# Token rows of the first expert step by products with zero-one tiles instead of a gather

## The chip, the core and the metric

The kernel runs on one core of one Trainium2 chip. The metric is the device time of one execution in microseconds (us). A core has five engines that run beside each other and wait for each other by semaphores: TensorE (PE in the profile; PEld is its weight load), VectorE (DVE), ScalarE (ACT), GpSimd (POOL) and SyncE (SP). Here SP issues the loads of weights, POOL the loads and stores of token rows and of modulation vectors. All transfers run on the core's 16 DMA engines.

## What is computed

One step of a two-layer streaming encoder over 512 prompt tokens and 32 sample tokens, width 1024, all in float32. Each layer ends in a mixture of experts: 16 experts in 4 groups, two experts for each token, both from its best group.

```python
def _moe(h, w_router, b_router, w_gate, w_up, w_down):
    logits = jnp.einsum('btd,de->bte', h.astype(jnp.float32), w_router.astype(jnp.float32))
    scores = jax.nn.softmax(logits, axis=-1)
    ...
    for e in range(N_EXPERTS):
        act = jax.nn.silu(h @ w_gate[e]) * (h @ w_up[e])
        term = combine[..., e:e + 1] * (act @ w_down[e])
        y = term if y is None else y + term
    return y
```

The first layer's mixer pools over trailing tokens, the second's is attention over shared keys and values. Between them lie projections; in front of all of it, products of the conditioning vector with the adaLN weights give shift, scale and gate vectors.

## The kernel before

**Tiles.** The 544 tokens are `NT` = 5 tiles of 128 rows (the last has 32). `h` holds the normed tokens, one token to a partition. `pb[0..7]` are the PSUM banks.

**Routing.** `pick` on DVE finds each token's two experts; PE (`ranks`) counts, and DVE (`places`) computes from the counts the row of each token in a list sorted by expert. These row numbers are `posf[:, 0, r, t]` (r is the first or second expert, t the tile) and, cast to integers, `posi`; with the cast the semaphore `rows_ready` rises. `places` then goes on with tables (which expert stands where, which rows belong to a step, the rows to gather results from) and ends with `pos_ready`.

**Dispatch.** On POOL, `dispatch` waits for `rows_ready` and scatters `h` into the list `xs_d` in device memory by ten indirect transfers (`scattered`). After that and `pos_ready` it loads the rows of a step: `load_x(n)` brings 128 rows of `xs_d` into `xg[n % 2]`.

**Expert loop.** 13 steps (`NSTEP`) in each layer, with 128 rows of one expert or 64 rows each of two experts (`PATTERN`: B is one expert, P two). For a step, PE transposes the rows (`pe_tx`, into `pb[0]` and `pb[1]`), ACT and DVE copy one half each into `xgT` (`copy_x`), and PE multiplies by the gate weights, the up weights, transposes the activations and multiplies by the down weights. PE's order is written out in `experts`: up of step n, transposes and half of the gate of step n+1, transposed activations of n, the other half of the gate, down of n. Steps are numbered g through both layers.

**Order on each engine.** Each engine runs its instructions in the order of the code. On DVE that is `pick`, `places`, in the first layer three additions `stage_ada` for the last adaLN groups, then the loop's copies. On PE in the first layer the last adaLN groups, `ada(5)` and `ada(6)`, stand behind `ranks`, and the loop begins when `ada_staged` says that the last of them is added. On SP the weights of the first two steps come first; in the first layer the last four of these six loads wait until the rows of step 1 have landed (`xg_loaded[1]`). Later loads go into slots of `ring` as PE frees them.

**Memory that is shared.** `xg`, `xgT`, `sg` and `hact` lie over `h`: they may be written once the scatter has read it. `mod` holds the modulation vectors of a stage; `load_ab(2)` fills it for the next stage, with five loads on POOL.

The gather in `dispatch`, which the change moves and cuts:

```python
pool.wait_ge(scattered, 16 * 2 * NT * (layer + 1))
pool.wait_ge(pos_ready, layer + 1)
b = layer * NSTEP
load_x(0)
load_x(1)
if layer == 0:
    load_ab(2)
```

and the wait on SP in the first layer: `if layer == 0 and n == 2: sp.wait_ge(xg_loaded[1], 16)`.

Of the kernel before, what the change touches and what calls it, by code (L numbers as in the profile page):

```python
# [12 lines left out]
def bass_yoco_stream_step(  # L13
# [96 lines left out]
    with ctx:  # L110
# [26 lines left out]
        hactT = hT_raw[:, 0:512].rearrange("p (k t) -> p k t", k=KE)  # L137
        ysb = hT_raw[:, 512:2560].rearrange("p (b n) -> p b n", b=2)
        pair_w = hT_raw[:, 2560:3072].rearrange("p (a i j) -> p a i j", a=2, i=NE)

# [12 lines left out]
        partT_f = rf[:, 13312:13312 + TOK]  # L153
        mf = mod[:, :, :, :].rearrange("p a s d -> p (a s d)")
        PT = rf[:, 23552:24576].rearrange("p (b n) -> p b n", b=2)

# [127 lines left out]
        rows_ready = sem("rows_ready")  # L284
        pos_ready = sem("pos_ready")
        scattered = sem("scattered")
        xg_loaded = [sem(f"xg{i}_loaded") for i in range(2)]
# [225 lines left out]
        def _(pool):  # L513
# [102 lines left out]

            def dispatch(layer):
                pool.wait_ge(rows_ready, layer + 1)
                pool.wait_ge(tail_stored, 16)
# [17 lines left out]
                b = layer * NSTEP  # L637
                load_x(0)
                load_x(1)
                if layer == 0:  # L640
                    load_ab(2)

                for n in range(NSTEP):
                    if layer == 0 and n == NSTEP - 2:
                        for j in range(0, NOV, TP):
                            m = min(TP, NOV - j) * P
                            g.dma_start(ys_d[(NSTEP + j) * P:(NSTEP + j) * P + m, :], x_prompt[0, 0:m, :]).then_inc(rows_filled, 16)
                    if n + 2 < NSTEP:
                        pool.wait_ge(E.tx, 2 * (b + n) + 2)
                        load_x(n + 2)  # L650
                    pool.wait_ge(E.ys_act, b + n + 1)
                    pool.wait_ge(E.ys_dve, b + n + 1)
                    par = (b + n) % 2
                    g.dma_start(ys_d[n * P:n * P + P, :], ysb[:, par, :]).then_inc(y_stored[par], 16)  # L654
# [75 lines left out]
        def _(pe):  # L730
# [74 lines left out]
            def pe_tx(g, par):  # L805

                for half, done in enumerate((E.xt_act, E.xt_dve)):
# [4 lines left out]
                    last.then_inc(E.tx, 1)  # L812

            def tile_product(bank, lhs, rhs, start, stop):

                if len(rhs) == 1:
                    return T.matmul(bank[:, :], lhs, rhs[0], start=start, stop=stop)  # L817
                for a in range(2):
                    last = T.matmul(bank[HALF * a:HALF * a + HALF, :], lhs[:, HALF * a:HALF * a + HALF], rhs[a],  # L819
                                    start=start, stop=stop, tile_position=(0, HALF * a))  # L820
                return last

            def pe_gate(g, par, ws, ks):
                for k in ks:
                    if k == 0:
                        pe.wait_ge(E.xt_act, g + 1)
                        pe.wait_ge(E.xt_dve, g + 1)
                        if g:
                            pe.wait_ge(E.silu, g)
                    last = tile_product(pb[3], xgT[:, par, k, :], [w[:, k * DE:(k + 1) * DE] for w in ws],  # L830
                                        k == 0, k == KC - 1)
# [3 lines left out]
            def pe_up(g, par, ws):  # L835
                if g:
                    pe.wait_ge(E.hact, g)
                for k in range(KC):
                    last = tile_product(pb[4], xgT[:, par, k, :], [w[:, k * DE:(k + 1) * DE] for w in ws],
                                        k == 0, k == KC - 1)  # L840
                last.then_inc(E.up, 1)

            def pe_th(g):
                pe.wait_ge(E.hact, g + 1)
                for c in range(KE):
                    last = T.transpose(pb[2][:, c * P:(c + 1) * P], hact[:, c:DE:KE], ident[:, :])
                last.then_inc(E.th, 1)
# [12 lines left out]
            def experts(layer):  # L860
# [8 lines left out]
                def tokens(n):  # L869
                    g = b + n  # L870
                    loads = sum(len(STEP_PLACES[i % NSTEP]) for i in range(g % 2, g + 1, 2))
                    pe.wait_ge(xg_loaded[g % 2], 16 * loads)
                    pe_tx(g, g % 2)

                tokens(0)
                pe_gate(b, b % 2, units(G_SLOT, 0), range(KC))
# [267 lines left out]
        def _(act):  # L1144
# [84 lines left out]
            def experts(layer):  # L1229
                b = layer * NSTEP  # L1230

                def copy_x(g):
                    act.wait_ge(E.tx, 2 * g + 1)
                    if g >= 2:
                        act.wait_ge(E.up, g - 1)
                    A.activation(xgT[:, g % 2, 0:4, :], pb[0][:, :].rearrange("p (c t) -> p c t", c=4),  # L1236
                                 ACT.Copy).then_inc(E.xt_act, 1)

                copy_x(b)
                for g in range(b, b + NSTEP):  # L1240
                    act.wait_ge(E.gate, g + 1)
                    if g:
                        act.wait_ge(E.hact, g)
                    A.activation(sg, pb[3][:, :], ACT.Silu).then_inc(E.silu, 1)
                    if g + 1 < b + NSTEP:
# [200 lines left out]
        def _(dve):  # L1446
# [162 lines left out]
            def places(layer):  # L1609
# [20 lines left out]
                tt(selv[:, :, :], rank[:, :, :], bc(offs[:, :], NT, 1), ALU.add)  # L1630
                picked(0, selv).then_inc(rows_ready, 1)


# [50 lines left out]
            def experts(layer):  # L1684
                b = layer * NSTEP

                def copy_x(g):
                    dve.wait_ge(E.tx, 2 * g + 2)
                    if g >= 2:
                        dve.wait_ge(E.up, g - 1)  # L1690
                    V.tensor_copy(xgT[:, g % 2, 4:8, :], pb[1][:, :].rearrange("p (c t) -> p c t", c=4)).then_inc(E.xt_dve, 1)  # L1691

                copy_x(b)
                for g in range(b, b + NSTEP):
                    dve.wait_ge(E.silu, g + 1)
                    dve.wait_ge(E.up, g + 1)
                    if g:
                        dve.wait_ge(E.th, g)
                    V.tensor_tensor(hact, pb[4][:, :], sg, ALU.mult).then_inc(E.hact, 1)  # L1699
                    if g + 1 < b + NSTEP:  # L1700
# [309 lines left out]
```

## Time and profile before

| what | value |
|---|---|
| median of 3 runs | 1463.25 us (1459.91 to 1463.81) |
| the profiled execution | 1463.11 us |
| its span in the trace | 1461.6 us |
| PE busy | 1168.8 us, 80% of the span |
| DVE busy | 447.4 us, 31% |
| ACT busy | 237.4 us, 16% |
| POOL busy | 148.0 us, 10% |
| chain that ended last | PE 71%, DVE 12%, DMA 9%, issue 3% |
| DMA | 365 MB, mean 250 GB/s |

The page lists busy time by engine, the span in slices, the queues, the chain of work that ended last and the costliest groups of instructions. A busy share is a mean over stages with different limits; what a stage is worth is read from the chain and the timeline of that stage. In a group, "out<-in" names the tiles; the last part is the idle time of the engine just before, with what ended most of it. `h<-xs_d` is the load of token rows: `xg` lies in `h`. Line 811 is the transposes of the rows, 817 and 819 the expert products (one or two experts), 744 the adaLN products, 1691 DVE's copy of the transposed rows.

### The profile page before, as it was taken

The numbers are of one execution on the slowest core, as the hardware profiler recorded it, in microseconds if no ns is written. First come the engines' busy times: TensorE is split into PE (matmuls) and PEld (weight loads), VectorE is DVE, ScalarE is ACT, GpSimd is POOL, SyncE is SP. The second block draws the span as 40 slices with busy tenths as digits, with TensorE's granted clock in tenths as the row PEclk, the third lists the DMA queues.
The fourth block names the chain that finished last, engine by engine and source line by source line (L and its number), as shares of the span: only waits on it lengthen the run. The fifth ranks groups of instructions, "written<-read, shape, count | busy, mean of one in ns | idle before, by whom it ended". The sixth has DMA issues, their size and how long they took to land.

```text
span 1461.6 us, 13678 instructions
## 1 busy us (share of the span) xinstructions
PE 1168.8 (80%) x4952; PEld 605.7 (41%) x4952; DVE 447.4 (31%) x1023; ACT 237.4 (16%) x517; POOL 148.0 (10%) x280
## 2 busy tenths in 40 slices
PE   2559748899999965999995888779934999999990
PEld 0027314344344422444554777555422444344340
DVE  1144640001010018264146677222363000101005
ACT  2002101010101004112123444211120001010101
POOL 6100030000000011000003000201003000000002
PEclk9869868999999986999997899779966999999996
DMA  9999799999998972311425000817035799899835
GB/s 320 400 388 353 272 403 380 392 430 348 386 402 331 381 274 80 109 58 61 181 58 161 0 0 0 253 55 298 0 133 205 282 421 379 354 428 346 346 135 197
DMA packets 55233, 365.44 MB, mean 250 GB/s; under 512 B 7215, under 2 KB 7711, under 8 KB 36156
## 3 DMA queue, kind: packets, MB, share of 16 engines
q1 hardware_dynamic: 32512, 285.79, 49.9%
q0 software_dynamic: 21104, 78.40, 15.4%
q8 instruction: 35, 0.57, 0.2%
q10 hardware_dynamic: 1564, 0.53, 0.1%
q14 instruction: 18, 0.15, 0.0%
HBM read 335.09 MB, written 34.33 MB: 253 GB/s over the span
## 4 chain that ended last, share of the span: by engine, by line
PE 71%; DVE 12%; DMA 9%; issue 3%; POOL 2%; ACT 1%; SPq 0%; ACTq 0%; DVEq 0%; POOLq 0%
PE pb L817 28%; PE pb L982 15%; PE pb L819 9%; PE pb L1076 2%; DMA ring<-in_ada_w_dram 2%; PE pb L758 2%; PE pb L811 2%; PE pb L1053 1%; DMA ring<-in_w_gate_dram 1%; DMA gainb<-in_norm_g_dram 1%; PE pb L1121 1%; POOL xs_d L622 1%; DMA ada_d<-stage 1%; DVE h L1691 1%; DVE ring L1887 1%
## 5 line engine op out<-in xcount | busy, mean ns | idle before, releaser
L817 PE MATMUL pb<-ring,h 128*128 128x512 f32 x640 | 289.2, 601 | 19.7 <-DVE h L1691 19.7
L982 PE MATMUL pb<-ring,hT_raw 128*128 128x512 f32 x512 | 226.8, 601 | 1.3 <-DVE hT_raw L1508 0.8
L817 PEld LDWEIGHTS pb<-ring,h 128*128 128x128 f32 x640 | 119.6, 192 | 162.2 <-issue 162.2
L982 PEld LDWEIGHTS pb<-ring,hT_raw 128*128 128x128 f32 x512 | 97.4, 193 | 117.6 <-issue 116.5
L817 PE MATMUL pb<-ring,hT_raw 128*128 128x512 f32 x320 | 143.1, 600 | 1.5 <-issue 1.5
L1705 DVE COPY hT_raw<-pb 128x512 f32<-128x512 f32 x26 | 18.0, 692 | 383.5 <-PE pb L817 293.7
L744 PE MATMUL pb<-ring,cT 128*32 128x512 f32 x448 | 72.4, 787 | 68.1 <-DMA ring<-in_ada_w_dram 55.3
L819 PE MATMUL pb<-ring,h 128*64 128x512 f32 x384 | 88.1, 606 | 9.1 <-DVE h L1691 4.9
L817 PEld LDWEIGHTS pb<-ring,hT_raw 128*128 128x128 f32 x320 | 60.7, 192 | 80.5 <-issue 80.5
L1699 DVE TENSOR_TENSOR h<-pb,h 128x512 f32<-128x512 f32 x26 | 18.0, 692 | 182.3 <-PE pb L817 143.9
L654 POOL DMA_DIRECT2D ys_d<-hT_raw x26 | 14.1, 543 | 577.0 <-DVE hT_raw L1705 577.0
L1236 ACT ACTIVATE h<-pb 128x512 f32<-128x512 f32 x26 | 15.5, 597 | 312.6 <-PE pb L811 312.6
L744 PEld LDWEIGHTS pb<-ring,cT 128*32 128x32 f32 x448 | 15.6, 130 | 118.2 <-DMA ring<-in_ada_w_dram 56.8
L1076 PE MATMUL pb<-ring 128*128 x320 | 48.2, 284 | 18.2 <-DVE ring L1902 18.2
L758 PE MATMUL pb<-ident,h 128*128 128x128 f32 (+1 forms) x160 | 28.0, 325 | 42.1 <-DVE h L1503 32.0
L811 PE MATMUL pb<-ident,h 128*128 128x128 f32 x208 | 29.7, 288 | 34.5 <-DMA h<-xs_d 34.5
L1076 PEld LDWEIGHTS pb<-ring 128*128 128x128 f32 x320 | 42.7, 199 | 24.4 <-DVE ring L1902 22.3
L819 PEld LDWEIGHTS pb<-ring,h 128*64 128x64 f32 x384 | 27.7, 138 | 60.0 <-issue 59.3
L811 PEld LDWEIGHTS pb<-ident,h 128*128 128x128 f32 x208 | 27.7, 193 | 49.1 <-DMA h<-xs_d 24.8
L1387 ACT ACTIVATE ring<-ring,mx 128x128 f32<-128x128 f32 (+1 forms) x64 | 36.0, 563 | 60.0 <-DVE mx L1892 60.0
L758 PEld LDWEIGHTS pb<-ident,h 128*128 128x128 f32 (+1 forms) x160 | 23.5, 200 | 51.9 <-DVE h L1503 37.5
L819 PE MATMUL pb<-ring,hT_raw 128*64 128x512 f32 x192 | 42.5, 595 | 0.0
(318 smaller groups left out, 1268.9 us busy)
## 6 DMA issues: line engine op xcount, KB each, us to landing
ring<-in_w_gate_dram SPq DMA_DIRECT2D x32, 2048.0 KB, 10.6
ring<-in_w_up_dram SPq DMA_DIRECT2D x32, 2048.0 KB, 11.9
ring<-in_w_down_dram SPq DMA_DIRECT2D x32, 2048.0 KB, 12.4
ring<-in_ada_w_dram SPq DMA_DIRECT2D x24, 2048.0 KB, 10.5
ys_d<-hT_raw POOLq DMA_DIRECT2D x26, 512.0 KB, 10.6
h<-xs_d POOLq DMA_DIRECT2D x20, 512.0 KB, 15.5
ring<-in_kv_ada_w_dram SPq DMA_DIRECT2D x4, 2048.0 KB, 11.2
ring<-in_w_kvf_dram SPq DMA_DIRECT2D x4, 2048.0 KB, 16.9
```

The lines of the kernel that those rows point to most:

```text
L622: g.indirect_dma_start(out=xs_d[:, :], out_offset=bass.IndirectOffsetOnAxis(ap=posi[0:rows[t], 0, r, t:t + 1], axis=0), in_=h[0:rows[t], t ...
L744: last = T.matmul(bank[32 * j:32 * j + 32, :], cT[:, 2 * u + k, :], w[:, k, j, :], start=(u == 0 and k == 0), stop=(u == 3 and k == 1), ti ...
L758: last = T.transpose(pb[2 + b][:, c * P:c * P + rows[t]], half_cols(src, t, 4 * b + c), ident[0:rows[t], 0:rows[t]])
L811: last = T.transpose(pb[half][:, c * P:(c + 1) * P], xg[:, par, 4 * half + c:D:KC], ident[:, :])
L817: return T.matmul(bank[:, :], lhs, rhs[0], start=start, stop=stop)
L819: last = T.matmul(bank[HALF * a:HALF * a + HALF, :], lhs[:, HALF * a:HALF * a + HALF], rhs[a], start=start, stop=stop, tile_position=(0, H ...
L982: last = T.matmul(bank[:, :], hT[:, k, col[t]:col[t] + P], w[:, k * 512:(k + 1) * 512], start=(k == 0), stop=(k == KC - 1))
L1076: last = T.matmul(pb[6 + n % 2][:, 0:HD], PT[:, n % 2, c * P:(c + 1) * P], vv[:, c, bass.ds(j * 2 * HD + s * HD, HD)], start=(c == 0), sto ...
L1236: A.activation(xgT[:, g % 2, 0:4, :], pb[0][:, :].rearrange("p (c t) -> p c t", c=4), ACT.Copy).then_inc(E.xt_act, 1)
L1387: A.activation(S_sb[:, n % 4, 0:w], S_sb[:, n % 4, 0:w], ACT.Exp, bias=mx[:, n, 2:3], accum_out=rs[:, n, 0:1]).then_inc(at_exp, 1)
L1699: V.tensor_tensor(hact, pb[4][:, :], sg, ALU.mult).then_inc(E.hact, 1)
L1705: V.tensor_copy(ysb[:, g % 2, 512:1024], pb[6][:, :]).then_inc(E.ys_dve, 1)
```

## The change

The first step of each layer (step 0 and step 13) no longer reads its rows from `xs_d`. Since the list is sorted, its rows are those with numbers 0 to 127. DVE builds for each token tile a 128x128 tile `oneh` with a one where a token's row number (`posf`, either expert) equals the column; POOL writes the column numbers `iotap`. PE then computes the transposed rows as products: for each of 8 column groups of `h`, five products over the token tiles add up in PSUM (`pe_pick`). The first step's `xgT`, `sg` and `hact` get buffers of their own in `mod` (`xgT0`, `sg0`, `hact0`), as `h` is still needed by the scatter. `oneh` and `iotap` lie in `hT_raw`. The scatter stays. `load_x(0)` is gone, `load_x(1)` waits for the products, and `load_ab(2)` moves into the loop, behind the first step's use of `mod`.

```diff
+        oneh = hT_raw[:, 3072:3072 + NT * P].rearrange("p (t n) -> p t n", t=NT)
+        iotap = hT_raw[:, 3072 + NT * P:3072 + NT * P + P]
...
+        xgT0 = mf[:, 0:1024].rearrange("p (k t) -> p k t", k=KC)
+        sg0, hact0 = mf[:, 1024:1536], mf[:, 1536:2048]
+
+        def step_xgT(g):
+            return xgT[:, g % 2, :, :] if g % NSTEP else xgT0
...
             def dispatch(layer):
+                pool.wait_ge(logits_done, layer + 1)
+                g.iota(iotap[:, :], pattern=[[1, P]], base=0, channel_multiplier=0,
+                       allow_small_or_imprecise_dtypes=True).then_inc(iota_ready, 1)
                 pool.wait_ge(rows_ready, layer + 1)
...
                 b = layer * NSTEP
-                load_x(0)
+                pool.wait_ge(E.tx, 2 * b + 2)
                 load_x(1)
-                if layer == 0:
-                    load_ab(2)
 
                 for n in range(NSTEP):
+                    if layer == 0 and n == 2:
+                        pool.wait_ge(E.th, b + 1)
+                        pool.wait_ge(E.up, b + 1)
+                        load_ab(2)
...
+            def pe_pick(g):
+
+                pe.wait_ge(picks_ready, g // NSTEP + 1)
+                for half, done in enumerate((E.xt_act, E.xt_dve)):
+                    if g:
+                        pe.wait_ge(done, g)
+                    for c in range(4):
+                        for t in range(NT):
+                            last = T.matmul(pb[half][:, c * P:(c + 1) * P], h[0:rows[t], t, 4 * half + c:D:KC],
+                                            oneh[0:rows[t], t, :], start=(t == 0), stop=(t == NT - 1))
+                    last.then_inc(E.tx, 1)
...
-                    loads = sum(len(STEP_PLACES[i % NSTEP]) for i in range(g % 2, g + 1, 2))
+                    loads = sum(len(STEP_PLACES[i % NSTEP]) for i in range(g % 2, g + 1, 2) if i % NSTEP)
...
-                tokens(0)
+                pe_pick(b)
                 pe_gate(b, b % 2, units(G_SLOT, 0), range(KC))
...
                 picked(0, selv).then_inc(rows_ready, 1)
+                dve.wait_ge(iota_ready, layer + 1)
+                for t in range(NT):
+                    last = V.tensor_scalar(oneh[:, t, :], iotap[:, :], posf[:, 0, 0, t:t + 1], None, ALU.is_equal)
+                link(last)
+                for t in range(NT):
+                    last = V.scalar_tensor_tensor(out=oneh[:, t, :], in0=iotap[:, :], scalar=posf[:, 0, 1, t:t + 1],
+                                                  in1=oneh[:, t, :], op0=ALU.is_equal, op1=ALU.add)
+                last.then_inc(picks_ready, 1)
```

The uses of `xgT`, `sg` and `hact` in PE's products, ACT's and DVE's copies become `step_xgT(g)`, `step_sg(g)` and `step_hact(g)`.

## Rows read from the trace of the kernel before

**Rows 1.** The page's groups: line, engine, tiles, count, busy, mean, idle before.

```profile
L811 PE MATMUL pb<-ident,h 128*128 128x128 f32 x208 | 29.7, 288 | 34.5 <-DMA h<-xs_d 34.5
```

**Rows 2.** Chain that ended last, second layer: start us, us, what.

```profile
1107.42 3.58 DMA xs_d<-h,posi
...
1112.29 3.76 DMA h<-xs_d
...
1118.11 0.70 DVE h L1691
...
1119.06 15.41 PE pb L817 x32
```

**Rows 3.** The same chain, first layer.

```profile
210.27 10.80 DMA h<-xs_d
...
224.02 15.78 PE pb L817 x32
...
249.44 18.45 DMA ring<-in_w_gate_dram
267.99 5.35 PE pb L819 x16
...
301.34 7.02 PE pb L819 x32
```

**Rows 4.** Timeline, second layer, DVE: start us, us, engine, line, operation, tiles.

```profile
1095.20 0.17 DVE L1627 CAST posi<-posf 128x10 int32<-128x10 f32 x1
...
1108.68 0.18 DVE L1682 CAST tabi<-tabf 1x49 int32<-1x49 f32 x1
```

**Rows 5.** Timeline, first layer, DVE and PE; in brackets idle before and releaser.

```profile
200.66 1.29 DVE L1469 TENSOR_TENSOR stage<-pb,adab 128x512 f32<-128x512 f32 x2
...
201.41 9.92 PE L744 MATMUL pb<-ring,cT 128*32 128x512 f32 x64 [12.81 <-DVE stage L1469]
...
211.50 0.69 DVE L1469 TENSOR_TENSOR stage<-pb,adab 128x512 f32<-128x512 f32 x1 [9.55 <-PE pb L744]
```

**Rows 6.** Groups by line and shape, DVE: busy us, mean ns, idle before.

```profile
L1478 DVE TENSOR_TENSOR bands<-bands,hT_raw 128x128 f32<-128x128 f32 x4 | 1.2, 293 | 0.1
...
L1476 DVE TENSOR_SCALAR hT_raw<-hT_raw 128x128 f32<-128x128 f32 x4 | 0.9, 226 | 0.1
...
L1638 DVE TENSOR_SCALAR cap<-order 128x16 f32<-128x16 f32 x2 | 0.8, 405 | 0.1
```

**Rows 7.** Timeline of PE in the pooling mixer: products with h tiles.

```profile
105.31 0.63 PE L942 MATMUL pb<-bands,h 128*128 128x128 f32 x2
105.74 0.64 PE L945 MATMUL pb<-bands,h 128*128 128x128 f32 x2
...
108.70 0.39 PE L945 MATMUL pb<-bands,h 128*128 128x128 f32 x2
108.92 0.39 PE L942 MATMUL pb<-bands,h 128*128 128x128 f32 x2
```

**Rows 8.** Stretches: busy us of PE, PEld, DVE, ACT, POOL; clock, DMA share, GB/s.

```profile
208.00:212.00 4.00, 3.33 (x32) 0.72 (x24) 0.50 (x1) 0.00 (x0) 1.14 (x3) 1.00 0.99 415
...
232.00:236.00 4.00, 4.00 (x11) 1.81 (x10) 0.00 (x0) 0.60 (x1) 0.00 (x0) 1.00 1.01 313
252.00:256.00 4.00, 4.00 (x11) 1.76 (x10) 0.00 (x0) 1.08 (x2) 0.00 (x0) 1.00 1.02 430
```

**Rows 9.** Timeline of SP, first layer: issues of weight loads.

```profile
222.25 0.33 SPq L401 DMA_DIRECT2D ring<-in_w_gate_dram  x1
...
284.70 0.33 SPq L401 DMA_DIRECT2D ring<-in_w_down_dram  x1
```

**Rows 10.** Single transfers issued at 205.1, 284.7, 286.0: size, us from issue to landing.

```profile
ring<-in_w_gate_dram SPq DMA_DIRECT2D x1, 2048.0 KB, 8.5
...
ring<-in_w_down_dram SPq DMA_DIRECT2D x1, 2048.0 KB, 12.7
...
ys_d<-hT_raw POOLq DMA_DIRECT2D x1, 512.0 KB, 10.7
```

More of the change, by code:

```diff
@@ L154, in bass_yoco_stream_step, with step_sg, step_hact @@
         mf = mod[:, :, :, :].rearrange("p a s d -> p (a s d)")
+        xgT0 = mf[:, 0:1024].rearrange("p (k t) -> p k t", k=KC)
+        sg0, hact0 = mf[:, 1024:1536], mf[:, 1536:2048]
+        def step_xgT(g):
+            return xgT[:, g % 2, :, :] if g % NSTEP else xgT0
+        def step_sg(g):
+            return sg if g % NSTEP else sg0
+        def step_hact(g):
+            return hact if g % NSTEP else hact0
         PT = rf[:, 23552:24576].rearrange("p (b n) -> p b n", b=2)
@@ L285, in bass_yoco_stream_step @@
         pos_ready = sem("pos_ready")
+        picks_ready = sem("picks_ready")
+        iota_ready = sem("iota_ready")
         scattered = sem("scattered")
@@ L829, in pe_gate @@
                             pe.wait_ge(E.silu, g)
-                    last = tile_product(pb[3], xgT[:, par, k, :], [w[:, k * DE:(k + 1) * DE] for w in ws],
+                    last = tile_product(pb[3], step_xgT(g)[:, k, :], [w[:, k * DE:(k + 1) * DE] for w in ws],
                                         k == 0, k == KC - 1)
@@ L838, in pe_up @@
                 for k in range(KC):
-                    last = tile_product(pb[4], xgT[:, par, k, :], [w[:, k * DE:(k + 1) * DE] for w in ws],
+                    last = tile_product(pb[4], step_xgT(g)[:, k, :], [w[:, k * DE:(k + 1) * DE] for w in ws],
                                         k == 0, k == KC - 1)
@@ L845, in pe_th @@
                 for c in range(KE):
-                    last = T.transpose(pb[2][:, c * P:(c + 1) * P], hact[:, c:DE:KE], ident[:, :])
+                    last = T.transpose(pb[2][:, c * P:(c + 1) * P], step_hact(g)[:, c:DE:KE], ident[:, :])
                 last.then_inc(E.th, 1)
@@ L1235, in copy_x @@
                         act.wait_ge(E.up, g - 1)
-                    A.activation(xgT[:, g % 2, 0:4, :], pb[0][:, :].rearrange("p (c t) -> p c t", c=4),
+                    A.activation(step_xgT(g)[:, 0:4, :], pb[0][:, :].rearrange("p (c t) -> p c t", c=4),
                                  ACT.Copy).then_inc(E.xt_act, 1)
@@ L1243, in experts @@
                         act.wait_ge(E.hact, g)
-                    A.activation(sg, pb[3][:, :], ACT.Silu).then_inc(E.silu, 1)
+                    A.activation(step_sg(g), pb[3][:, :], ACT.Silu).then_inc(E.silu, 1)
                     if g + 1 < b + NSTEP:
@@ L1690, in copy_x @@
                         dve.wait_ge(E.up, g - 1)
-                    V.tensor_copy(xgT[:, g % 2, 4:8, :], pb[1][:, :].rearrange("p (c t) -> p c t", c=4)).then_inc(E.xt_dve, 1)
+                    V.tensor_copy(step_xgT(g)[:, 4:8, :], pb[1][:, :].rearrange("p (c t) -> p c t", c=4)).then_inc(E.xt_dve, 1)
                 copy_x(b)
@@ L1698, in experts @@
                         dve.wait_ge(E.th, g)
-                    V.tensor_tensor(hact, pb[4][:, :], sg, ALU.mult).then_inc(E.hact, 1)
+                    V.tensor_tensor(step_hact(g), pb[4][:, :], step_sg(g), ALU.mult).then_inc(E.hact, 1)
                     if g + 1 < b + NSTEP:
```

## The prediction

> **What bounds the kernel now.** I read four views in this order. The page first: TensorE (PE) carries the chain nearly everywhere, and its group for the token transposes, L811, has 34.5 us of idle time that ended on the gathered rows, `h<-xs_d` [rows 1]. Then the chain of waits, to see where that time lies. There are two places, the first step of each layer's expert loop. In the second layer the rows are asked for at 1112.29 and take 3.76 us, VectorE (DVE) copies their transposed half at 1118.11, and the gate product starts at 1119.06 [rows 2]. In the first layer they are asked for at 210.27, take 10.80 us, and the gate product starts at 224.02; later the chain leaves PE for the weights: the gate weights of step 2, issued at 249.44, take 18.45 us, and PE goes on at 267.99 [rows 3]. Third, the timeline of DVE and PE just before: who is free, and when, once the rows no longer decide [rows 4, 5]. Last, stretches with the granted clock and the DMA rate, and the SyncE (SP) queue, which feeds the weights [rows 8, 9].
>
> The sum is made against the profiled execution: 1463.1 us, of which 1461.6 are the span. The median shown is 1463.25, so a gain carries over one to one.
>
> **What the change removes.** Only the gather of the first step: two of 32 loads (0.5 MB each). The scatter stays, since step 1 reads from it, and its 20 issues still start right after the cast that makes the row numbers, at 1095.4 in the second layer [rows 4].
>
> **What it adds, and where it lies.**
> *The zero-one tiles.* Five comparisons and five compare-and-adds on 128x128 stand on DVE between the row numbers and the rest of `places`. Nearest rows: a TENSOR_SCALAR of that shape 226 ns, a TENSOR_TENSOR 293 ns [rows 6]. Sum 5 x 0.226 + 5 x 0.293 = 2.6 us; I take 3.0 for the wait between the two groups and the start of each. All that DVE still has to do in `places` moves later by as much, and so does what waits on its end. A gain here is excluded: the work is new and in order. The iota on GpSimd (POOL) comes before a wait that ends much later, and costs nothing.
> The row that speaks for a higher price is L1638: a TENSOR_SCALAR on 128x16 that takes 405 ns, though the 128x128 one takes 226 [rows 6]; it runs while POOL writes scatter descriptors, as the new ones will. If each of the five comparisons lost 0.24 us so, the tiles would cost 4.2 us. The Trainium skill (GPSIMD Engine Reference, 1. Specifications) says that POOL's way to SBUF is shared with DVE and contended by DVE work that uses two ports or two SBUF inputs. By that rule all ten additions are of the contended sort; row L1638 agrees, the two 128x128 rows, taken while POOL issued no scatter, can't show it.
> *The products.* Forty products 128x128 replace eight transposes. The same form, an h tile as weights and a 128-column constant tile, two products accumulating, runs in the pooling mixer: two products every 0.43 us while the clock is low (105.31 to 105.74) and every 0.22 us once it is high (108.70 to 108.92) [rows 7]. So the pick costs 39 x 0.111 + 0.3 = 4.7 us at full clock, 39 x 0.214 + 0.4 = 8.7 at half.
>
> **Second layer.** The tiles are ready at about 1098.4, and PE is idle: even at half clock the products end at 1107.1. They don't set the time. The copy of the second half of the rows stands on DVE *behind* `places`, whose last cast (L1682) ends at 1108.86 [rows 4], now 3.0 later, 1111.9. From the start of that copy to the gate product is 0.95 us [rows 2]. New start 1108.86 + 3.0 + 0.95 = 1112.8 instead of 1119.06: **6.2 us gained**, though the rows stop waiting 14 us earlier. With tiles of 2.6 to 4.2 us the gain is 6.6 to 5.0. PE has then been idle some 5 us, so the clock is low again, as before; no gain there. The next cover: rows of step 1 are asked for only after `places` and the pick, about 1113.1, and land 3.8 us later (5 if beside another), by 1118; PE wants them after gate and up, 15.41 us after its start [rows 2], at 1128. Hidden with 10 us to spare. All six weight tiles of the first two steps were asked for long before.
>
> **First layer.** PE has other work between: the last adaLN products start when DVE has done `places` and a staging add (201.41, after 12.81 idle), and the expert loop waits for the last staging add, 211.50 + 0.69 [rows 5]. All of that is 3.0 later. The pick then starts at 215.3, and as PE paused only 1 us, at full clock: the granted clock was 1.00, that is 2.4 GHz, in 208 to 212 [rows 8]. Pick 4.7, copy 0.9: the gate product starts at 220.9 instead of 224.02, and the two products take 14.0 us warm instead of 15.78 [rows 3]: PE is 4.9 us ahead.
> But this stage is bound by the weights. SP holds four weight loads back until the rows of step 1 have landed (before: 222.25 [rows 9]). Those rows now wait for the pick: POOL stands in that wait, with all later row loads behind it. 220.0 + 1.3 (POOL from the end of its wait to the load, as from 1111.00, where the scatter lands, to 1112.29 [rows 2]) + 3.8 = 225.1, so 2.9 us later than before, and the DMA engines run dry from about 221. Against that, nothing else is queued then: the gather of step 0 and the five vector loads (1.8 MB) that ran in 212 to 233 are gone or moved. One load from a free queue takes 8.5 us [rows 10], each further one 2.1 MB / 430 GB/s = 4.9 us [rows 8]. The gate weights of step 2 are the seventh: 225.1 + 8.5 + 6 x 4.9 = 263.0, with 1 MB of rows and results between, 265.3. Before: 267.9. PE would be ready at 264.9 - 4.9 = 260, so the weights still decide: **2.7 us gained** (1.5 to 4.9, the latter being PE's own lead).
> *The moved vector loads.* `load_ab(2)` now stands on POOL in step 2, ahead of the row load of step 4; its conditions have long been met. Its 1.84 MB are 4.3 us of DMA at 430 GB/s, or 5.9 at the 313 GB/s of 232 to 236, where it ran before [rows 8]. PE-bound steps hide it as far as the weights have slack: the second down weights of step 2, issued at 284.70, land 12.7 us later at 297.4, and PE needs them at 301.34 [rows 3, 9, 10], slack 3.9. So it costs 0 to 2.0 us. A result store issued right after took 10.7 us where a load of its size alone takes 3.8 [rows 10, 2], so it stood behind the weights issued before it, and only later weights would feel the vectors: I take 0.6. The Trainium skill (DMA: Bandwidth & Descriptors, Queues, rings and completion order) says that each DMA engine takes turns between queues, packet by packet. By that rule the vectors would also slow the weights already queued, the cost would be 2.0 and the total 1456.2; the store's row speaks against it.
> First layer: 2.7 - 0.6 = **2.1 us**. After it the loop is PE-bound in both layers and carries its shift to the end.
>
> **Sum:** 1463.1 - 6.2 - 2.1 = 1454.8.
>
> **Rivals.**
> *Pick at half clock in the first layer.* If the one idle microsecond, or the 128-column products themselves, leave the clock low, the pick takes 8.7 instead of 4.7; every microsecond goes into the held weights. First layer 2.1 - 4.0 = -1.9: 1458.8. For: the clock rose only late in the adaLN products. Against: the full clock in 208 to 212 [rows 8].
> *Weights no longer late.* If the free queue brings the seventh load by 260 and the vectors hide, the first layer gains all 4.9: 1463.1 - 6.2 - 4.9 = 1452.0. Against: it needs nearly nothing beside the weights.
> *Contended tiles.* 4.2 us instead of 3.0: second layer 5.0, first 0.9, total 1457.2. This is the mechanism of row L1638; the skill's rule on shared SBUF access, above, is its general form.
> *Slower: the held queue.* Place: SP's wait for the rows of step 1 in the first layer. Each microsecond by which they land after 225.1 delays the weights by one. If they take 10.8 us, as the first step's did behind other transfers [rows 3], instead of 3.8, and the pick 8.7, SP goes on at 236.1, the gate weights of step 2 land at 276.3, the first layer loses 8.9 with the vectors, and the total is 1463.1 - 6.2 + 8.9 = 1465.8. It decides from 8.3 us of delay on (SP after 233.4). Against: SP itself holds the transfers that would stand in front.
>
> **How the numbers follow.** Forecast 0.50 (1452.5 to 1457), half clock 0.25 (1457 to 1461), weights in time 0.12, contended tiles 0.08, held queue 0.05. Likeliest 1454.8. The range 1451.5 to 1459.5 leaves out most of the held queue, the slow end of the half clock and some of the fast case. A measurement tells 0.3% from no change, 4.4 us: below 1458.9 lie the forecast, half of the half-clock case, the fast case and nearly all of the contended one, 0.81; slower than 1467.6 only the worse part of the last, 0.03; the rest, 0.16, is the same.
>
> **What would show it.** In the second layer PE's first gate product 17.4 us after the cast of the row numbers instead of 23.7, its wait ending on DVE's copy, which starts right behind the L1682 cast; the products done 4 us or more before. In the first layer 40 products from 215, SP's four loads released near 225, DMA engines dry just before, and a wait of 4 to 5 us on the gate weights of step 2. I am wrong if DVE's part after the tiles turns out not to stand in front of the copy, if the pick runs at another clock, or if PE waits for weights in steps 2 to 4.

## The result, and the profile after

The changed kernel takes 1499.59 us (median of 4 runs, 1497.31 to 1502.6), the kernel before 1463.53 beside it: a ratio of 1.0253, 95% interval 1.0224 to 1.0281. The change makes the kernel slower by 36 us; the forecast was 8 us faster. The profiled execution took 1497.53 us, 1496.0 of it the span, 34.4 more than before.

The chain of waits of the kernel after, first layer (start us, us, what):

```profile
217.04 23.66 PE pb L844 x80
...
241.56 15.87 PE pb L851 x32
...
267.07 20.91 DMA ring<-in_w_gate_dram
288.07 6.17 PE pb L853 x16
...
310.45 37.82 DMA h<-xs_d
348.31 1.98 PE pb L833 x8
```

L844 is the pick, L851 and L853 are the gate, up and down products, L833 the transposes of the later steps. Three rows carry the loss: the pick takes 23.66 us in 80 instructions; the gate weights of step 2 let PE start at 288.07 where it was 267.99 [rows 3]; and a new wait has appeared, on the row load of step 4. In the kernel before that load, and the transposes that use it, stood so (timeline, POOL and PE; in brackets idle before and releaser):

```profile
287.14 0.54 POOL L633 DMA_DIRECT2D h<-xs_d  x1 [0.61 <-issue]
```
```profile
315.26 1.04 PE L811 MATMUL pb<-ident,h 128*128 128x128 f32 x8
```

PE had no idle time there before. After, the timeline of POOL, and of PE at the end of the wait:

```profile
307.50 0.54 POOL L609 DMA_DIRECT2D mod<-ada_d  x1
...
309.57 0.57 POOL L615 DMA_DIRECT2D gainb<-in_kv_norm_dram  x1
310.45 0.53 POOL L653 DMA_DIRECT2D h<-xs_d  x1 [0.31 <-issue]
```
```profile
348.31 1.97 PE L833 MATMUL pb<-ident,h 128*128 128x128 f32 x8 [12.00 <-DMA h<-xs_d]
```

The five moved vector loads (L609 to L615) now stand right ahead of the rows of step 4 on POOL's queue. The second layer, again the chain:

```profile
1125.92 0.17 DVE posi L1661
1126.10 0.98 DVE hT_raw L1668 x5
...
1127.10 1.41 DVE hT_raw L1671 x5
...
1128.56 23.90 PE pb L844 x80
1152.48 0.70 DVE mod L1733
...
1153.42 2.04 PE pb L851 x2
```

From the cast of the row numbers to the gate product it is 27.5 us; before it was 1119.06 - 1095.20 = 23.9 [rows 2, 4]. Taking the lag behind the kernel before at each mark gives the accounting: 3.2 us already at the first layer's cast (190.24 against 187.07), ahead of the change's first work on DVE and PE; 17.5 at its gate product; 20.1 at the gate products of step 2; 33.0 at the transposes of step 4 (348.31 against 315.26); 35.6 one product later (356.43 against 320.79), as PE came out of the wait at a granted clock of 0.50 (348 to 352) and took 5.33 us for a gate product that took 3.67 before; 30.7 at the second layer's cast; 34.4 at its gate product and at the end.

The lag stays at 35.6 us to the end of the first layer's loop. The 5 us that come back lie in the second layer's attention, which both kernels compute alike: 345.2 us from 697.05 on before, 340.2 from 732.52 on after. In 20 us of it the granted clock was 0.83 before (797 to 817) and 1.00 after (832 to 852). Over the profiles of all the kernels here this stretch takes 337.5 to 345.2 us, whether they hold the change or not, so a comparison of two single profiles is uncertain by some microseconds there.

### The profile page after: what moved, and what is told of

Same layout as the page of the kernel before. It is cut to its first block, busy times and chain, and to the rows that moved or that the text cites. A ratio compares the mean times of both kernels' runs of the same rounds, so it can differ in the third digit from the quotient of the medians.

```text
span 1496.0 us, 13977 instructions
## 1 busy us (share of the span) xinstructions
PE 1214.3 (81%) x5096; PEld 642.9 (43%) x5096; DVE 451.8 (30%) x1043; ACT 237.1 (16%) x517; POOL 145.8 (10%) x280
## 4 chain that ended last, share of the span: by engine, by line
PE 71%; DVE 13%; DMA 10%; issue 3%; ACT 1%; POOL 1%; SPq 0%; DVEq 0%; ACTq 0%; POOLq 0%
PE pb L851 27%; PE pb L1016 15%; PE pb L853 8%; PE pb L844 3%; DMA h<-xs_d 3%; DMA ring<-in_ada_w_dram 2%; PE pb L1110 2%; PE pb L780 2%; PE pb L833 1%; DMA ring<-in_w_gate_dram 1%; DVE ring L1929 1%; DMA gainb<-in_norm_g_dram 1%; PE pb L766 1%; DMA ada_d<-stage 1%; PE pb L1155 1%
## 5 line engine op out<-in xcount | busy, mean ns | idle before, releaser
L851 PE MATMUL pb<-ring,h 128*128 128x512 f32 x576 | 259.7, 599 | 17.7 <-DVE h L1733 17.7
L851 PEld LDWEIGHTS pb<-ring,h 128*128 128x128 f32 x576 | 106.9, 191 | 144.4 <-issue 144.4
L851 PE MATMUL pb<-ring,hT_raw 128*128 128x512 f32 x320 | 143.1, 600 | 1.5 <-issue 1.5
L853 PE MATMUL pb<-ring,h 128*64 128x512 f32 x384 | 88.9, 611 | 11.5 <-DMA ring<-in_w_gate_dram 6.6
L851 PEld LDWEIGHTS pb<-ring,hT_raw 128*128 128x128 f32 x320 | 60.7, 192 | 80.5 <-issue 80.5
L853 PEld LDWEIGHTS pb<-ring,h 128*64 128x64 f32 x384 | 27.7, 140 | 63.3 <-issue 62.5
L844 PE MATMUL pb<-hT_raw,h 128*128 128x128 f32 (+1 forms) x160 | 47.5, 470 | 7.3 <-DVE hT_raw L1671 6.3
L844 PEld LDWEIGHTS pb<-hT_raw,h 128*128 128x128 f32 (+1 forms) x160 | 40.5, 330 | 14.8 <-DVE hT_raw L1671 6.5
L853 PE MATMUL pb<-ring,hT_raw 128*64 128x512 f32 x192 | 42.5, 595 | 0.0
## 6 DMA issues: line engine op xcount, KB each, us to landing
ring<-in_w_down_dram SPq DMA_DIRECT2D x32, 2048.0 KB, 12.6
```

Source lines behind the costliest of these rows:

```text
L844: last = T.matmul(pb[half][:, c * P:(c + 1) * P], h[0:rows[t], t, 4 * half + c:D:KC], oneh[0:rows[t], t, :], start=(t == 0), stop=(t == NT ...
```

## The experiments

Two theories stood against each other at each of three places: what made the pick dear, who paid for the moved vectors, and what SP's wait did.

**Neighbouring weight columns.** In the pick the columns that go to PE as weights are every eighth of `h`; in the mixer [rows 7] they are neighbours.

```diff
-  h[0:rows[t], t, 4 * half + c:D:KC],
+  h[0:rows[t], t, (4 * half + c) * P:(4 * half + c + 1) * P],
```

> The changed kernel, but the forty products of the first step take 128 neighbouring columns of an h tile as weights instead of every eighth column (so the first step multiplies the wrong columns; the work is the same). Theory A, every eighth column makes the weight loads slow: the 80 passes (two for a product) go at 0.11 to 0.21 us each, as in the pooling mixer, so 9 to 17 us instead of 23.7 in each layer; the first layer gains what the pick loses in length, the second at most 10.5 (then DVE's places decide): 1474 to 1487 us instead of 1499.6. Theory B, the length comes from the low granted clock or from adding up five products in one PSUM region: the pick stays at 20 us or more and the time within 6 us of 1499.6.

Measured: 1482.2 us, ratio 1.0154 (1.0099 to 1.021). The chain's two picks:

```profile
215.57 12.10 PE pb L844 x80
...
1111.13 21.89 PE pb L844 x80
```

With neighbouring columns the first layer's pick takes half as long. In the second layer only 2 us came back: another cause remained there. Stretches of the two picks (us of PE, PEld, DVE, ACT, POOL with instructions, then granted clock, DMA share, GB/s):

```profile
216.00:220.00 4.00, 4.00 (x29) 3.35 (x27) 0.00 (x0) 0.00 (x0) 0.00 (x0) 1.00 0.93 369
...
1116.00:1120.00 4.00, 4.00 (x15) 3.33 (x16) 3.52 (x15) 0.00 (x0) 3.08 (x4) 0.50 0.97 377
```

The first ran at the full clock throughout, the second at half.

**The vectors.** Three kernels: the change with `load_ab(2)` in step 11 instead of step 2; the kernel before with only `load_ab(2)` moved to step 2; the change without SP's wait for the rows of step 1.

```diff
-                    if layer == 0 and n == 2:
+                    if layer == 0 and n == NSTEP - 2:
                         load_ab(2)
```

> The changed kernel with the five vector loads (load_ab(2)) on POOL moved from step 2 to step 11, behind all row loads. Theory A, the vectors stand ahead of the row load of step 4 on POOL's queue, and each takes its turn with the weights: PE's wait of 12.0 us on the rows of step 4 goes, 1486 to 1488 us. Theory B, those rows are late because the weights, held back and now all asked for at once, fill the DMA engines, whoever stands ahead: 8 us or more of the wait stay, 1494 us or more.

Measured: 1482.67 us, ratio 1.0144 (1.0106 to 1.0183). PE no longer waits for the rows of step 4. The gain of 17 us is 5 more than that wait: PE also waited 2 us less for the gate weights of step 2, 4.6 instead of 6.6, and the 2.6 us that the low clock cost right behind the wait are gone with it.

```diff
 # the kernel before
-                if layer == 0:
-                    load_ab(2)
                 for n in range(NSTEP):
+                    if layer == 0 and n == 2:
+                        load_ab(2)
```

> The kernel before with one part of the change alone: load_ab(2) on POOL in step 2 of the first layer, ahead of the row load of step 4. Theory A (as above): the row load of step 4 lands some 20 us later than before and PE waits some 10 us for it; the gate weights of step 2 come up to 4 us sooner, as the vectors no longer run ahead of them: 1467 to 1471 us. Theory B, the view of the prediction, that only later weights feel the vectors: 1459 to 1463 us, no wait on the rows of step 4.

Measured: 1476.62 us, ratio 1.0087 (1.0057 to 1.0118), worse than expected. The chain, and PE's timeline after it:

```profile
287.31 38.56 DMA h<-xs_d
```
```profile
325.92 1.33 PE L811 MATMUL pb<-ident,h 128*128 128x128 f32 x5 [12.63 <-DMA h<-xs_d]
```

Neither theory named the size. The move alone, without any pick, costs 13.9 us (1476.62 against 1462.73). In the profile PE is 2.1 us ahead at the transposes of step 3 (289.48 against 291.61), waits 12.63 us for the rows of step 4, and is 13.8 us behind one product later (334.61 against 320.79), as the gate product behind the wait takes 5.86 us instead of 3.67. How the load of half a megabyte comes to 38 us, the DMA queues between 290 and 325 show (queue: packets, MB, share of the engines' time):

```profile
q1 hardware_dynamic: 778, 11.44, 81.0%
q0 software_dynamic: 784, 2.76, 20.0%
```

q1 are SP's weights, q0 is POOL's. They got as many packets each, but a packet of POOL's is 2.76 / 784 = 3.5 KB and one of SP's 14.7 KB. POOL's queue moved 2.76 MB in 35 us, 79 GB/s; the vectors and the rows, 1.84 + 0.52 MB, take 30 us at that rate, and the store issued ahead of them 7 more.

```diff
-                    if layer == 0 and n == 2:
-                        sp.wait_ge(xg_loaded[1], 16)
```

> The changed kernel without SP's wait for the rows of step 1 in the first layer: the four weight loads go out as soon as their slots are free. Theory A, the held queue makes the gate weights of step 2 late: they land before PE wants them, the 6.6 us wait in front of step 2 goes, and with a less crowded queue part of the 12.0 us wait on the rows of step 4: 1485 to 1493 us. Theory B, the DMA rate sets that landing whenever SP asks: 1497 us or more.

Measured: 1494.13 us, ratio 1.0221 (1.0185 to 1.0258). The chain:

```profile
282.42 3.65 PE pb L851 x16
...
302.26 38.02 DMA h<-xs_d
340.33 1.98 PE pb L831 x8
```

The wait for the gate weights of step 2 is gone (PE reaches its gate products at 282.42, behind DVE's copy), the pick stays (23.62 and 23.90), and the wait for the rows of step 4 does not shrink: 12.2 us, where theory A expected less. SP's wait was worth 5 us here.

**The pick alone, and without most of its products.**

> The changed kernel with load_ab(2) in step 11 and without SP's wait for the rows of step 1. Theory A, three separate costs, which add up: what is left is the long pick alone, 14 us of late start less the 4 us wait for weights of the kernel before in the first layer, 3.6 us in the second: 1474 to 1479 us. Theory B, the held queue costs nothing that the late vectors don't mend as well: as with the late vectors alone, 1481 to 1484 us.

Both edits of above together. Measured: 1478.94 us, ratio 1.0105 (1.0075 to 1.0135); with every other new wait gone, the pick keeps the kernel slower by 15 us. The medians give rough shares of the 36 us: 16.9 for the vectors (1499.59 to 1482.67), 3.7 for SP's wait once the vectors are late (to 1478.94), 15.8 for the pick (to 1463.1 for the kernel before).

```diff
-                        for t in range(NT):
+                        for t in range(1):
...
-                                            oneh[0:rows[t], t, :], start=(t == 0), stop=(t == NT - 1))
+                                            oneh[0:rows[t], t, :], start=True, stop=True)
```

> The changed kernel with two edits: the pick takes only the first of the five token tiles (8 products instead of 40; the rows of the other tiles are left out), and load_ab(2) stands in step 11. Theory A, the prediction's structure was right and only the pick's price and the place of the vectors were wrong: 16 passes take 3 to 5 us, in the second layer DVE's end of places decides again and the gate product starts 17.4 us after the cast of the row numbers instead of 23.7; in the first layer the gate weights of step 2 come some 3 us sooner: 1452 to 1457 us. Theory B, something else in the change costs as well (tiles, buffers, the held queue): 1459 us or more.

Measured: 1453.82 us, ratio 0.9927 (0.9899 to 0.9956). The chain, and DVE's and PE's timeline in the second layer:

```profile
215.04 4.09 PE pb L844 x16
219.99 13.97 PE pb L851 x32
```
```profile
1108.58 0.18 DVE L1724 CAST tabi<-tabf 1x49 int32<-1x49 f32 x1
1108.68 0.67 DVE L1733 COPY mod<-pb 128x512 f32<-128x512 f32 x1
```
```profile
1109.61 2.90 PE L851 MATMUL pb<-ring,mod 128*128 128x512 f32 x3 [10.04 <-DVE mod L1733]
```

With a pick of 4.1 us the forecast's picture appears: DVE's copy starts right behind its last cast, the gate product follows 16.9 us after the cast of the row numbers (1092.74), 0.5 less than forecast, and the first layer's stands at 219.99 (forecast 220.9). But the first layer's weights do not follow the forecast:

```profile
267.90 6.50 PE L853 MATMUL pb<-ring,h 128*64 128x512 f32 x16 [9.83 <-DMA ring<-in_w_gate_dram]
```

SP went on at 224.91, as forecast (225.1), and PE waited 9.8 us for the gate weights of step 2, until 267.90; the forecast had 4 to 5 us and 265.3, the kernel before 267.99.

**What a pass costs.** Both kernels leave out the fifth tile's products, which have 32 rows; the first has neighbouring weight columns too.

```diff
-                        for t in range(NT):
+                        for t in range(4):
...
-  start=(t == 0), stop=(t == NT - 1))
+  start=(t == 0), stop=(t == 3))
```

> The kernel with neighbouring weight columns again, and of its five products per column group only the four with full token tiles: the 32 tokens of the fifth tile are left out of the first step's rows, and its columns are the wrong ones as in the kernel it is made from. 64 passes of TensorE per layer instead of 80. Question: what is left between the pick's price per pass with neighbouring columns (12.10 / 80 = 0.151 us at full clock, 21.89 / 80 = 0.274 at half) and that of the pooling mixer (0.111 and 0.214). Theory A: the price belongs to every pass of such a product; the pick takes 64 x 0.151 = 9.7 us in the first layer and 64 x 0.274 = 17.5 in the second, the time is 1474 to 1478. Rival B: the 32-row product that ends each group carries the surplus; the full tiles run as in the mixer, 64 x 0.111 = 7.1 us and 64 x 0.214 = 13.7, the time is 1467 to 1472. I give A 0.6.

> The change under study with the 32-row product that ends each group left out (the fifth tile's 32 tokens are missing from the first step's rows); the weights keep their stride of eight columns. 64 passes per layer. With neighbouring columns and the same 64 passes the pick took 7.42 us in the first layer, 0.116 a pass; with 16 strided passes it took 4.08, 0.255 a pass. Theory A: the stride alone makes a pass 0.25 to 0.27 us, 64 of them 16 to 17.5 us in each layer, and the granted clock falls to 0.5 in the course of the first layer's pick as in the change; the time is 1481 to 1487. Rival B: the 32-row products carry most of it, the strided full tiles take 0.12 to 0.18 us a pass, 8 to 11 us, the clock stays at 1.00; the time is 1469 to 1476. I give A 0.85.

Measured: 1469.49 us and 1476.79 us, one execution each, so the traces say more here than the times. PE's timelines, neighbouring columns first, then the stride, the first layer's pick and the second's:

```profile
216.80 7.41 PE L844 MATMUL pb<-hT_raw,h 128*128 128x128 f32 x64 [0.92 <-DVE stage L1503]
...
1111.22 9.44 PE L844 MATMUL pb<-hT_raw,h 128*128 128x128 f32 x64 [6.33 <-DVE hT_raw L1671]
```
```profile
214.59 15.50 PE L844 MATMUL pb<-hT_raw,h 128*128 128x128 f32 x64 [0.92 <-DVE stage L1503]
```
```profile
1119.22 15.55 PE pb L844 x64
```

The rival won the first of the two: full tiles at 0.116 us a pass, the mixer's pace, so the 16 short passes carried the surplus. In the second price and time are between the two theories: 0.242 a pass, a little under A's 0.25, but the clock did not fall, as B said. The weight loads tell the stride: line, passes, then minimum, median and maximum ns of one, neighbouring columns and every eighth:

```profile
L844 PEld LDWEIGHTS pb<-hT_raw,h x128: 186/192/333, 216.8 to 1120.3; 128*128 128x128 f32 x128
```
```profile
L844 PEld LDWEIGHTS pb<-hT_raw,h x128: 312/336/338, 214.6 to 1134.2; 128*128 128x128 f32 x128
```

The Trainium skill (SBUF — State Buffer, Door 1: The DMA port swizzle) says that SBUF is read by lines of 16 bytes and that each access to a new line is penalised; a stride of eight float32 is 32 bytes, and 336 against 192 ns agrees. At a granted clock of 0.50 the difference is nearly gone: in the second layer's picks of the kernel after and of the one with neighbouring columns a load took 334 and 333 ns in the median.

Second layer, the first stretches of the pick: neighbouring columns, then the stride, both without 32-row products:

```profile
1112.00:1116.00 4.00, 4.00 (x23) 4.00 (x22) 3.52 (x15) 0.00 (x0) 3.09 (x4) 0.56 0.90 357
1116.00:1120.00 4.00, 4.00 (x38) 4.00 (x38) 3.48 (x16) 1.88 (x2) 3.09 (x4) 1.00 0.97 375
```
```profile
1120.00:1124.00 4.00, 4.00 (x19) 4.00 (x19) 3.52 (x15) 0.00 (x0) 3.09 (x4) 0.56 0.90 357
1124.00:1128.00 4.00, 4.00 (x19) 4.00 (x18) 3.49 (x15) 0.81 (x2) 3.09 (x4) 1.00 0.97 376
```

From the low to the full clock the neighbouring columns go from 23 to 38 passes in 4 us; the strided ones stay at 19. So the stride's price hides the clock's: a strided pass over a full tile costs 0.24 us at either.

Where the short products lose their time shows in the weight loads of the kernel after, second layer:

```profile
1130.77 0.55 PEld L844 LDWEIGHTS pb<-hT_raw,h 32*128 32x128 f32 x2 [0.22 <-issue]
...
1131.54 2.00 PEld L844 LDWEIGHTS pb<-hT_raw,h 128*128 128x128 f32 x8 [0.22 <-issue]
```

Before each pair of 32-row loads, and again before the next full tile, loading stops for 0.22 us. Without the 32-row products it never stops (PEld busy 4.00 of 4.00 above).

The clock in the first layer, by stretches: the kernel after, with one of its second layer as the last line, then the strided pick without 32-row products:

```profile
216.00:220.00 4.00, 3.08 (x15) 2.72 (x11) 0.69 (x1) 0.00 (x0) 0.00 (x0) 1.00 1.05 451
220.00:224.00 4.00, 4.00 (x15) 3.55 (x16) 0.00 (x0) 0.00 (x0) 0.00 (x0) 0.69 0.52 221
224.00:228.00 4.00, 4.00 (x16) 3.34 (x15) 0.00 (x0) 0.00 (x0) 0.00 (x0) 0.50 0.00 0
...
1144.00:1148.00 4.00, 4.00 (x16) 3.56 (x16) 0.00 (x0) 0.00 (x0) 0.00 (x0) 0.50 0.00 0
```
```profile
216.00:220.00 4.00, 4.00 (x19) 4.00 (x18) 0.00 (x0) 0.00 (x0) 0.00 (x0) 1.00 0.93 396
220.00:224.00 4.00, 4.00 (x19) 4.00 (x18) 0.00 (x0) 1.48 (x2) 0.00 (x0) 1.00 0.02 10
224.00:228.00 4.00, 4.00 (x18) 4.00 (x18) 0.00 (x0) 0.40 (x1) 0.00 (x0) 1.00 0.00 0
```

After, the clock fell from 2.4 to 1.2 GHz in the middle of the pick, while PE was busy in every stretch; without the short products it held. In the second layer it stood at 0.50 through the whole pick of the kernel after, and with neighbouring columns too; in both kernels without short products it was 1.00 from some 5 us into the pick on. The short products alone don't settle it, though: with neighbouring columns the first layer's pick held them and kept 1.00 through its 12.1 us. The DMA engines are not what the clock follows: at 224 to 228 they were dry in both kernels above, at 0.50 in one and 1.00 in the other.

**A version that gains.** The operands swapped: the zero-one tile is the weights, 512 neighbouring columns of `h` stream past it, 20 passes instead of 80, then a copy and the old eight transposes. In the first layer these products stand ahead of the last adaLN products, in time in which PE waited. Once without SP's wait, once with it:

```diff
+                for half in range(2):
+                    for t in range(NT):
+                        last = T.matmul(pb[4 + half][:, :], oneh[0:rows[t], t, :],
+                                        h[0:rows[t], t, 512 * half:512 * half + 512],
+                                        start=(t == 0), stop=(t == NT - 1))
...
             ada(5, [2, 3])
+            pe_pick(0)
             ada(6)
```

> A version meant to gain: operands swapped (the zero-one tile as weights, 512 neighbouring columns of h streaming, 20 passes), so that the rows come out untransposed; ACT copies them, PE transposes them as before. In the first layer these products stand before the last adaLN group, in PE's idle time. load_ab(2) in step 11, no wait of SP for the rows of step 1, POOL's load of them waits for the products only. Theory A, a pass of 512 columns costs 0.43 us as the expert products do, 0.85 while the clock is low, 9 to 14 us in all, hidden in the first layer, ending with DVE's places in the second: first layer 8 to 10 us sooner, second 5 to 7: 1445 to 1451 us. Theory B, the clock stays low and the 17 us push the last adaLN group and the gate product: 1452 to 1460 us.

Measured: 1449.44 us, ratio 0.9927 (0.9898 to 0.9957). PE's timeline:

```profile
190.94 9.43 PE L842 MATMUL pb<-h,hT_raw 128*128 128x512 f32 x20 [2.77 <-DVE hT_raw L1689]
204.98 1.94 PE L767 MATMUL pb<-ring,cT 128*32 128x512 f32 x8 [4.61 <-DVE stage L1521]
```

The gate product starts at 217.67 in the first layer, 6.4 us sooner than before, and 16.9 us after the cast in the second, 7.0 sooner. The first layer's part is lost again: PE still waits 9.8 us for the gate weights of step 2, until 265.75, and the first products behind the first layer's loop start at 560.95, before at 559.65. The total is theory A's, its 8 to 10 us in the first layer are not.

> As the version with the operands swapped and the products in TensorE's idle time, but with SP's wait for the rows of step 1 kept as in the change under study, and the vector loads where the change has them or later. Without that wait the gate weights of step 2 landed at 265.75, with 9.8 us of waiting before. Theory A: the weights of the first layer are bound by bytes, and a wait of SP only leaves the queue empty for some us; here the row load is asked for near 212.8, SP goes on near 217, the gate weights of step 2 land at 266 to 270 and the time is 1449 to 1454. Rival B: what the prediction used, the weights land some 40 us after SP goes on, near 257, TensorE hardly waits, and the time is 1441 to 1446. I give A 0.6.

Measured: 1451.8 us, ratio 0.9942 (0.9923 to 0.9962). SP goes on at 220.48, later than either theory had it, and the weights land at 261.72: 41 us after SP, as rival B said, while the time is theory A's. The interval overlaps that of the version without the wait: which is better stays open. To see whether that version's gain is the pick's, the kernel before with the vectors in step 11 and without SP's wait:

```diff
 # the kernel before
-                        sp.wait_ge(xg_loaded[1], 16)
...
+                    if layer == 0 and n == NSTEP - 2:
                         load_ab(2)
```

> The kernel before with load_ab(2) in step 11 and without SP's wait, and no products: what of the last version's gain is not the pick's. Theory A: the rows of step 0 land no sooner (they wait for the scatter), so PE starts as before and only the 4 us wait for the gate weights of step 2 goes: 1457 to 1460 us. Theory B: the weights that are no longer held take turns with the rows of step 0, which land 3 to 8 us later: 1462 to 1467 us.

Measured: 1461.98 us, ratio 0.9994 (0.9971 to 1.0016). No difference: those two edits gain nothing by themselves, so the 0.7% need the swapped pick. That they add nothing beside it is not shown.

## Why the prediction was wrong

**The step that failed first: the price of the pick.** I priced 40 products at the pitch of [rows 7], 0.111 us at full clock and 0.214 at half, for 4.7 or 8.7 us. The pick took 23.66 and 23.90. Three errors add up to that, each measured by a kernel above:

- Rows 7 were read as two products each. Each is one: a float32 product is two passes, and the pitch of 0.22 us is that of a product. The trace of before could tell it. The group of L942 (line, passes, ns; first and last start; forms), which the prediction did not use, counts 80, but the mixer makes there 5 tiles x 8 column groups = 40 products:

```profile
L942 PE MATMUL pb<-bands,h x80: 271/275/582, 93.6 to 138.2; 128*128 128x128 f32 x64, 32*128 32x32 f32 x16
```

With 80 passes the sum would have been 80 x 0.116 = 9.3 us at full clock, 80 x 0.214 = 17.1 at half.

- The 32-row products. With neighbouring columns, 16 of them bring the first layer from 7.42 to 12.10 us, 0.29 a pass where a full tile takes 0.116, and the second from 9.44 to 21.89, as the clock then stays low.
- The stride. First layer 12.10 to 23.66; second 21.89 to 23.90. The full tiles take 8.1 of the first layer's 11.6 (7.42 to 15.52), the short ones and the fall of the clock the rest.

First layer: 4.7 + 4.6 + 2.8 + 11.6 = 23.7. Second: 8.7 + 8.4 + 4.8 + 2.0 = 23.9. My rival of a low clock in the first layer came true in part: the clock fell, 4 to 5 us into the pick. But its price, 8.7, was wrong by the same reading, and at this stride the fall cost little, since the first layer's pick, begun at 1.00, took 23.66 us and the second's, all at 0.50, 23.90. At the right price PE decides in the second layer, not DVE: `places` ended at 1141.94, the pick at 1152.46.

**The second step that failed: the moved vectors.** I put their cost at 0 to 2.0 us, and took 0.6, with the sentence that only later weights would feel them. It counted the slack of the weights alone. Behind the vectors on POOL's own queue stands the row load of step 4, whose slack is what decides: it was issued at 287.14 and wanted at 315.26, 28 us, and took 38. Measured: PE waits 12.6 us with the move alone and 12.0 in the change, and the move costs 13.9 us alone, 16.9 in the change. The store of 10.7 us [rows 10], from which I concluded that a POOL transfer stands behind the weights issued before it, fits the turn-taking as well. The rule that I set aside, of the Trainium skill (DMA: Bandwidth & Descriptors, Queues, rings and completion order), was the better guide: 784 packets against 778 agree with turns, packet by packet. But the price that I drew from it, 2.0 us on the weights, was as wrong: the turns favour the queue with the large packets, and the small ones wait.

**The slower rival** named the right place, SP's wait, and its formula held:

```profile
248.47 0.33 SPq L418 DMA_DIRECT2D ring<-in_w_gate_dram  x1
```

SP went on 26.2 us later than before [rows 9], and PE got the weights 39.6 us after that (forecast: 225.1 to 265.3, 40.2). Its chance, 0.05, was too low: of the 23.4 us by which SP was later than the forecast's 225.1, 19.0 are the pick's price, and 2.4 the row load, which took 6.2 us from its issue at 242.31 where the forecast had 3.8. Its time of 1465.8 holds neither that price nor the rows of step 4.

**What was right.** The tiles: five comparisons 1.06 us, five compare-and-adds 1.40, 2.5 in sum and not dearer beside POOL's scatter (forecast 3.0, up to 4.2). DVE's end of `places` as the bound of the second layer once the pick is short (7.0 us gained there, forecast 6.2), and the first layer's start: shown by the kernel with a fifth of the passes. That its 1453.8 us stand beside the forecast of 1454.8 is luck in part. It rests on the vectors' going to step 11. And the first layer's gain of 2.7 us on the weights is not there: SP went on in time, but the weights took 43.0 us from then instead of 40.2, so PE was 0.1 us ahead at step 2 and 1.2 behind at the end of the loop (528.58 against 527.37). The total makes up for it in the second layer's attention, 340.3 us in its profile and 345.2 in that of the kernel before, which has nothing to do with the change. The 3.2 us at the first layer's cast have no cause in the change either: over all the profiles the cast stands at 186.67 to 191.41, and at 188.64 in the kernel before with only the vectors moved, which runs the same code up to there as the 187.07. What makes it vary is open.

## What to carry to other kernels

Count the instructions of a group against the loops of the source before you take a pitch as the price of one product, and take it from a row with the same stride, the same number of rows and the same clock, not only the same form. When a load is moved on a queue, look for what stands behind it on that queue and take its slack, then the share that the queue gets beside the others. When a total agrees with a forecast, compare it stage by stage before you call the forecast right. A product that replaces a gather belongs in time in which the engine is idle, with the long neighbouring side streaming.

## What the runs showed of the hardware that was not expected

- Loading float32 weights of 128x128 from every eighth column took 336 ns, from neighbouring columns 192, both at full clock; passes came every 0.242 and 0.116 us. At half clock the loads took 334 and 333 ns, and strided passes came as often as at full clock (19 in 4 us).
- A short product (32 rows) is not cheaper than one of 128 rows but dearer when it stands between full ones: 0.29 us a pass against 0.116 in the first layer with neighbouring columns. At half clock the weight load stopped for 0.22 us before each pair of short loads and again behind it.
- The granted clock fell from 1.00 to 0.50 inside an unbroken run of strided passes that held 32-row products, and stayed at 1.00 in the same run without them. In the second layer it stayed at 0.50 in the picks with them, at either stride, and rose to 1.00 in those without. With neighbouring columns the first layer's pick kept 1.00 in spite of them. Why is open.
- With both queues full, POOL's got 784 packets to SP's 778 and 2.76 MB to 11.44: a load of half a megabyte behind five others took 38 us.
